# Self-attention: the softmax's division moved from the probabilities to the output block

## The reference, cut to what matters

```
s = jnp.einsum('bkgqd,bskd->bkgqs', q_blk, k).astype(jnp.float32) * scale
p = jax.nn.softmax(s, axis=-1).astype(v.dtype)
return jnp.einsum('bkgqs,bskd->bkgqd', p, v)
...
attn_branch = block_attention(q, k, v) @ w_attn_o
```

## Time and profile before

| | us |
|---|---|
| median of 3 runs | 2601.33 |
| lowest, highest | 2599.62, 2607.33 |
| profiled execution, its time | 2596.83 |
| its span | 2595.0 |

### The profile page before, as it was taken

One profiled execution on the slowest core, in us unless ns is written; L12 is line 12 of the kernel. 1 busy time (PEld: TensorE's weight loads), 2 busy tenths in 40 slices (PEclk: granted clock), 3 DMA queues, 4 the chain that ended last, 5 costly groups with the idle time before them and its releaser, 6 DMA issues.

```text
span 2595.0 us, 38678 instructions
## 1 busy us (share of the span) xinstructions
PE 2451.1 (94%) x13083; PEld 2070.5 (80%) x13083; DVE 2167.5 (84%) x3950; ACT 1101.6 (42%) x1943; POOL 1374.2 (53%) x1054
## 2 busy tenths in 40 slices
PE   7989999899989999999998889999999999999998
PEld 5767888788876778777866668888888888888887
DVE  6355544886779897877889978999999999999999
ACT  4464444333257313343317993333333333333333
POOL 0000000315832554745755547888887777777875
PEclk9999999999999999999999999999999999999999
DMA  6745545447974797877943559999999999999998
GB/s 249 267 139 179 195 146 181 174 189 262 381 270 119 290 333 289 337 271 254 387 167 134 211 223 391 414 415 415 415 415 415 415 414 415 415 415 394 415 415 317
DMA packets 240423, 787.50 MB, mean 303 GB/s; under 512 B 21905, under 2 KB 75329, under 8 KB 219553
## 3 DMA queue, kind: packets, MB, share of 16 engines
q0 software_dynamic: 112288, 408.77, 40.4%
q1 hardware_dynamic: 128000, 377.00, 39.0%
HBM read 728.01 MB, written 57.67 MB: 303 GB/s over the span
## 4 chain that ended last, share of the span: by engine, by line
PE 35%; DVE 23%; issue 20%; ACT 9%; DMA 9%; POOL 3%; POOLq 0%; DVEq 0%; SPq 0%; ACTq 0%
PE lin L245 9%; PE lin L247 9%; PE lin L246 9%; ACT row_ring L1866 4%; DVE Y L2494 3%; DVE w_lo L222 2%; DMA G<-in_downT 2%; DMA w_raw<-in_wall 2%; DVE rows L2480 2%; DVE row_ring L138 2%; DMA rows<-in_up,now 2%; DVE w_raw L2480 2%; DVE low L2460 2%; DVE low L2471 2%; PE tr L1795 2%
## 5 line engine op out<-in xcount | busy, mean ns | idle before, releaser
L150 POOL DMA_INDIRECT row_ring<-in_down,IDX x256 | 371.3, 1450 | 303.3 <-DVE dots L138 229.1
L222 DVE TENSOR_TENSOR w_lo<-w_raw,w_hi 128x2048 fp32r<-128x2048 f32 x100 | 229.2, 2292 | 218.5 <-ACT w_hi L214 214.1
L245 PE MATMUL lin<-w_hi,T_hi 128*128 128x512 f32 x976 | 389.0, 399 | 15.0 <-DVE w_lo L222 7.8
L247 PE MATMUL lin<-w_hi,T_lo 128*128 128x512 f32 x976 | 388.5, 398 | 0.0
L246 PE MATMUL lin<-w_lo,T_hi 128*128 128x512 f32 x976 | 386.1, 396 | 0.0
L214 ACT ACTIVATE w_hi<-w_raw 128x2048 fp32r<-128x2048 f32 x116 | 222.1, 1914 | 354.2 <-PE lin L247 331.5
L2353 POOL DMA_INDIRECT rows<-in_up,now x192 | 311.9, 1625 | 64.7 <-issue 56.8
L138 DVE CUSTOM_DVE_ANT_0 row_ring<-row_ring,H 128x1024 f32<-128x1024 f32 x256 | 303.0, 1223 | 37.9 <-DMA row_ring<-in_down,IDX 37.5
L245 PE MATMUL lin<-w_hi,c_hi 128*128 128x512 f32 x768 | 307.1, 400 | 15.9 <-DVE c_lo L2507 15.9
L2353 POOL DMA_INDIRECT w_raw<-in_up,now x189 | 274.2, 1451 | 84.2 <-issue 43.8
L245 PE MATMUL tr<-T_hi,w_hi 128*128 128x384 f32 x896 | 304.2, 340 | 2.2 <-DVE low L2460 2.2
(11 more groups left out here) (310 smaller groups left out, 5254.2 us busy)
## 6 DMA issues: line engine op xcount, KB each, us to landing
w_raw<-in_wall SPq DMA_DIRECT2D x116, 1024.0 KB, 6.8
row_ring<-in_up SPq DMA_DIRECT2D x128, 512.0 KB, 11.8
G<-in_downT SPq DMA_DIRECT2D x112, 512.0 KB, 11.3
wd<-dense_gates SPq DMA_DIRECT2D x32, 768.0 KB, 22.4
weight_rests<-w_lo SPq DMA_DIRECT2D x16, 1024.0 KB, 4.9
w_lo<-weight_rests SPq DMA_DIRECT2D x16, 1024.0 KB, 4.8
dense_gates<-peer SPq DMA_DIRECT2D x6, 2048.0 KB, 6.3
dense_gates<-w_raw SPq DMA_DIRECT2D x5, 2048.0 KB, 6.9
```

The lines of the kernel that those rows point to most:

```text
L150: pool.indirect_dma_start(self.ring[:, r % self.K, :], None, self.table, bass.IndirectOffsetOnAxis(ap=self.IDX[:, r:r + 1], axis=0)).then_ ...
L222: dve.tensor_tensor(self.lo[:, h % 2], self.raw[:, h % 2], self.hi[:, h % 2].bitcast(F32), ALU.subtract).then_inc(self.lo_done, 1)
L245: pe.matmul(out, lhs[0], rhs[0], start=start, stop=False, skip_group_check=True)
L247: return pe.matmul(out, lhs[1], rhs[0], start=False, stop=stop, skip_group_check=True)
```

## The change

The probabilities stay unnormalised. DVE's reciprocal and its two multiplications in every step go. Once for each block, DVE inverts all its sums (`invert`, in step `last + 1`), PE spreads the inverses over the block's 128 rows with small matmuls (`spread_factors`: the inverse of one tile and head, broadcast to 64 columns, as the stationary operand, the identity as the moving one), ACT copies the spread factors from the free bank of `tr` to `stage[2]`, DVE multiplies the block's output by them into `stage[0]` or `stage[1]`, ACT copies that into T_hi and DVE subtracts it for T_lo. The turn waits for the exponentials and no longer for DVE. The projection behind the attention no longer waits for all blocks at once but for each (`Blocks`). The background rows go to one in every step, and two in every third: 45 in the loop of the sample, where there were 26.

```
 class SelfAttention:
-    def norm(self, dve, p):
-        i = p % 3
-        dve.wait_ge(self.exped, 2 * p + 2)
-        dve.reciprocal(self.rr[:, i, :], self.rs[:, i, :]).then_inc(self.inverted, 1)
-        dve.wait_ge(self.inverted, p + 1)
-        for e in range(2):
-            dve.tensor_scalar(self.probs[:, i, e, 0:self.w], self.probs[:, i, e, 0:self.w], self.rr[:, i, e:e + 1], None,
-                              ALU.mult).then_inc(self.normed, 1)
+    def invert(self, dve, n):
+        nt = self.q.nt
+        dve.wait_ge(self.exped, 2 * nt * (n + 1))
+        dve.reciprocal(self.rr[:, n % 2, 0:nt, :], self.rs[:, n % 2, 0:nt, :]).then_inc(self.inverted, 1)
...
 def self_attention
+        LAG = 2 if q.nt == 4 else 3
+        last = [(hp + 1) * q.nt - 1 for hp in range(NH // 2)]
...
                 for e in range(2):
-                    pe.wait_ge(normed, 2 * p + e + 1)
+                    pe.wait_ge(exped, 2 * p + e + 1)
...
+            def spread_factors(n):
+                pe.wait_ge(att.inverted, n + 1)
+                if n >= 1:
+                    pe.wait_ge(scaled, n)
+                for t in range(q.nt):
+                    for e in range(2):
+                        product = pe.matmul(factors(n)[rows_of(e), t * P:(t + 1) * P],
+                                            att.rr[:, n % 2, t, e:e + 1].broadcast_to((P, HD)), ident[:],
+                                            start=True, stop=True, skip_group_check=True)
+                product.then_inc(valued, 1)
...
                 if step < N:
                     att.scores(pe, step)
+                for n, p in enumerate(last):
+                    if q.nt == 2 and step == p + LAG:
+                        spread_factors(n)
                 if 2 < step < N + 2:
                     turn(step - 2)
+                for n, p in enumerate(last):
+                    if q.nt == 4 and step == p + LAG:
+                        spread_factors(n)
                 if 3 <= step:
                     values(step - 3)
...
         @block.scalar
-                    if step == block_end[n] + 3:
-                        act.wait_ge(valued, 2 * block_end[n])
-                        act.activation(T[0][:, n, 0:w], tr[:, n % 2, 0:w], ACT.Copy).then_inc(out_hi, 1)
+                    if step == p + 3:
+                        act.wait_ge(valued, spread_done(n))
+                        if n == 0:
+                            spills_done(act)
+                        else:
+                            act.wait_ge(scaled, n)
+                        act.activation(factor(n), factors(n), ACT.Copy).then_inc(out_hi, 1)
+                    if step == p + 5:
+                        act.wait_ge(scaled, n + 1)
+                        act.activation(T[0][:, n, 0:w], out(n), ACT.Copy).then_inc(out_hi, 1)
...
         @block.vector
-                if 1 <= step < N + 1:
-                    att.norm(dve, step - 1)
-                if step % 4 != 0:
-                    bg.dve(dve, 1)
+                    if step == p + 1:
+                        att.invert(dve, n)
+                    if step == p + 4:
+                        dve.tensor_tensor(out(n), tr[:, n % 2, 0:w], factor(n), ALU.mult).then_inc(scaled, 1)
+                    if step == p + 6:
+                        dve.tensor_tensor(T[1][:, n, 0:w], out(n), T[0][:, n, 0:w].bitcast(F32),
+                                          ALU.subtract).then_inc(out_lo, 1)
+                if step < N + 4:
+                    bg.dve(dve, 2 if step % 3 == 0 else 1)
...
 def mixer_outputs
+            project_tokens(pe, st, H, 2, T, range(NT), lin, o, turn=blocks)
             attended(pe)
-            project_tokens(pe, st, H, 2, T, range(NT), lin, o)
```

More of the change, by code:

```diff
@@ L1074, in attention, with self_attention, factors, values_done @@
         return attended
-def self_attention(nc, block, q, bg, T, v_sb, ident, lin, tr, att, projected):
+def self_attention(nc, block, q, bg, T, v_sb, stage, ident, lin, tr, att, projected, spills_done):
     with ExitStack() as ctx:
         m = Pool(nc, ctx)
-        probs, rows_of, kv_of, normed, turned = att.probs, att.rows_of, att.kv_of, att.normed, att.turned
+        probs, rows_of, kv_of, exped, turned = att.probs, att.rows_of, att.kv_of, att.exped, att.turned
         pT = m.sb("att_probsT", [P, 2, 2, SAMPLE // P, P])
         copied, valued, out_hi, out_lo = (m.sem(f"att_{x}") for x in ("copied", "valued", "out_hi", "out_lo"))
+        scaled = m.sem("att_scaled")
+        LAG = 2 if q.nt == 4 else 3
         pairs, N, w = att.pairs, att.N, att.w
-        block_end = [(hp + 1) * q.nt for hp in range(NH // 2)]
+        last = [(hp + 1) * q.nt - 1 for hp in range(NH // 2)]
+        blocks = Blocks(out_lo)
+        def factors(n):
+            return tr[:, (n + 1) % 2, 0:w]
+        def values_done(p):
+            return 2 * (p + 1) + sum(x + LAG <= p + 3 for x in last)
+        def spread_done(n):
+            return 2 * (last[n] + LAG - 3) + n + 1
+        def fetched(n):
+            return 2 * n + 1
+        def hi_done(n):
+            return 2 * n + 2
+        def factor(n):
+            return stage[:, 2, 0:w]
+        def out(n):
+            return stage[:, n % 2, 0:w]
         @block.tensor
@@ L1096, in turn @@
                     for kb in range(q.nt):
-                        last = pe.transpose(lin[:, 4 + e, kb * P:(kb + 1) * P],
-                                            probs[:, p % 3, e, kb * P:(kb + 1) * P], ident[:])
-                    last.then_inc(turned, 1)
+                        product = pe.transpose(lin[:, 4 + e, kb * P:(kb + 1) * P],
+                                               probs[:, p % 3, e, kb * P:(kb + 1) * P], ident[:])
+                    product.then_inc(turned, 1)
             def values(p):
@@ L1129, in copy @@
                 if p >= 2:
[L1130 removed]
+                    act.wait_ge(valued, values_done(p - 2))
                 for e in range(2):
@@ L1167, in attended, with mixer_outputs @@
             eng.wait_ge(out_lo, NH // 2)
-        return attended
-def mixer_outputs(nc, block, st, q, bg, x_in, T, Y, G, lin, tr, A, U, GA, GS, ident, cleared, attended, spills_done):
+        return attended, blocks
+def mixer_outputs(nc, block, st, q, bg, x_in, T, Y, G, lin, tr, A, U, GA, GS, ident, cleared, attended, blocks, spills_done):
     NT, H = q.nt, q.h0 + 2 * W_AO
@@ L2575, in layer @@
                                                                    A, U, GA, GS, stage, ident, gains, *carried)
[L2576 removed]
+                        attended, blocks = self_attention(nc, block, q, bg, T, v_sb, stage, ident, lin, tr, att, projected,
+                                                          spills_done)
                     norm_m, mixed = mixer_outputs(
[L2578 removed]
+                        nc, block, st, q, bg, x_in, T, Y, G, lin, tr, A, U, GA, GS, ident, cleared, attended, blocks, spills_done)
                     with ExitStack() as c2:
```

56 lines of the change are left out of this document (33 added, 23 removed).

## The result

The changed kernel took 2613.23 us, median of 5 runs (2609.02 to 2617.14); the kernel before took 2601.33 us in 5 runs (2598.71 to 2607.33). The ratio is 1.0043, 95% interval 1.0025 to 1.0061: 11.9 us slower, where 2606 us, some 5 us slower, was forecast. The time lies inside the range and above the 0.3% bound. The profiled execution took 2609.02 us (span 2607.2), 12.2 us more than that of before.

A forecast was written before the change was run, and what follows sets the result against it. Two interleaved dependency rings (exponential, copies, turn, values, scores, maximum), no full engine, pace both loops. Sample +4.2, prompt +4.5, routing -3.6 give +5.1 us on 2596.83; 4.5 more for the median gives 2606 us, range 2595 to 2614.

The forecast's parts named there:

- rival B: Sample's loop: second rows of two-row steps delay the next maximum, +5.8 in place of 1.0, 2611 us; chance 0.20.
- +4.5 forecast: Prompt's loop: +5.4 us for seven longer blocks, less 0.9 of the projection's wait.
- 5.2 us against 4.43: Prompt's loop: a block takes 5.2 us, with PE itself in the dependency ring, against 4.43 before; +0.77.
- counted at -0.9: Prompt's loop end: the projection's wait of 0.97 us goes, 0.9 of it counted.
- +4.2 forecast: Sample's loop: 4.6 for seven blocks, +1.0 for the last block's spreading, -1.4 for the projection's wait.
- The spreading lies on the ring of the even steps: 14.26 us: Sample's loop: spreading between turn and values lengthens the even steps' dependency chain, 13.24 + 1.02 = 14.26 us a block.
- the other ring: Sample's loop: the odd steps' dependency chain, with two block copies on ACT in place of one, 14.20 us a block.
- 0.14 a block (1.0): Sample's loop: added for DVE in two-row steps with a block operation, 4.1 against 3.6 us; 7 x 0.14.
- +1.0 for the last spreading: Sample's loop end: the last block's spreading has no scores beside it to hide behind, +1.0 us.
- The projection's -1.4: Sample's loop end: the 1.45 us wait goes, since the projection's first half wants only blocks 0 to 3.
- -3.6 forecast: Routing: PE's 1.88 us wait and 1.68 us of slow clock go as 19 background rows leave.
- 0.6 us: Prompt's loop: one more TensorE drain per block from switching array tiling, 0.6 us over eight blocks, left out of the sum.

The follow-up runs named there:

- experiment 5: Changed kernel plus 20 dummy identity matmuls (4.4 us) in the pause before each loop's second turn; 2605.11 us, ratio 1.0013.
- experiment 12: Kernel before with blockwise projection, a background row in every step of the sample's loop and dummy matmuls in the pauses; 2592.71 us, ratio 0.9961.
- experiment 10: Kernel before with only the output projection waiting for blocks one by one; 2600.35 us, ratio 0.9991.
- Experiment 6: Changed kernel with only the first matmul of each block's spreading; 2608.46 us, ratio 1.0029.
- experiment 4: Changed kernel with 26 background rows in the sample's loop in place of 45; 2617.76 us, ratio 1.0063.
- in the second: Second trace, from the changed kernel run once more with nothing altered; 2617.54 us in one run.
- experiment 9: Kernel before with 34 dummy matmuls (8 us) ahead of the prompt's output projection; 2610.40 us, ratio 1.0037.
- experiments 3: Changed kernel with the sample's self-attention put back (normalised probabilities, 26 background rows), the prompt's as changed; 2616.44 us, ratio 1.0055.

## Why the prediction came out as it did

The sign of each part was right, and so were the prompt's block and the routing in size; by medians the loss was 11.9 us and not 5, and one step in the sample was right only in its number. That 2613 us lie in the range is partly luck: its upper end came from rival B, which came at a quarter of its price, and what carried the time there were the clock and a stretch that I had not priced.

*The prompt's loop, +4.5 forecast, +8.3 in the trace.* At full clock the loop takes 38.7 us (experiment 5) against 33.6 with the projection's wait (experiment 12): +5.1. The step "5.2 us against 4.43" holds to 0.03 us. But up to the last turn the loop loses only 4.6 us (199.43 - 164.01 = 35.42 against 195.74 - 164.91 = 30.83), not the 5.4 of seven blocks: the last two, which have few scores or none beside them, lose nothing (3.48 and 3.30 us between products, 4.25 and 2.75 between the T_lo before). The end, counted at -0.9, costs +0.5 (3.30 us from the last turn to the projection against 2.84): I had passed over it, and the last values wait 1.03 us for ACT. The remaining 3.2 us are clock. This is the term the sum lacked: I priced the loop as if the half-clock piece behind the pause had one length, and read 0.96 in the earlier trace rows as no concern of the change. With the new loop PE stands still 0.85 us in each block and the piece lasts 8.8 to 11.7 us; its cost is 3.3 to 4.7 us in place of 1.4 (1.9 in experiment 10). That keeping PE at work takes it away is shown; why the new loop keeps it longer, by its stalls or by its later matmuls, was not separated.

*The sample's loop, +4.2 forecast, +5.5 in the trace.* "The spreading lies on the ring of the even steps: 14.26 us" is the step that failed. What binds is the other ring: 13.24 + 2 x 0.48 = 14.20, with one block copy on each half of it. ACT's timeline of the changed kernel has both, three exponentials of the odd steps and three of the even ones:

```profile
795.07 0.69 ACT L660 ACTIVATE att_probs<-lin,att_sums 128x512 f32<-128x512 f32 x1 [0.66 <-DVE att_sums L665]
802.20 0.69 ACT L660 ACTIVATE att_probs<-lin,att_sums 128x512 f32<-128x512 f32 x1 [1.17 <-DVE att_sums L665]
809.30 0.69 ACT L660 ACTIVATE att_probs<-lin,att_sums 128x512 f32<-128x512 f32 x1 [0.69 <-DVE att_sums L665]
...
769.92 0.69 ACT L660 ACTIVATE att_probs<-lin,att_sums 128x512 f32<-128x512 f32 x1 [3.21 <-DVE att_sums L665]
777.41 0.69 ACT L660 ACTIVATE att_probs<-lin,att_sums 128x512 f32<-128x512 f32 x1 [1.47 <-DVE att_sums L665]
784.02 0.69 ACT L660 ACTIVATE att_probs<-lin,att_sums 128x512 f32<-128x512 f32 x1 [0.26 <-DVE att_sums L665]
```

The odd ones are 7.13 and 7.10 us apart, each 6.62 + 0.48 within 0.03: 14.23 us. The even ones are 7.49 and 6.61 us apart, 14.10 us: the spreading costs its ring 0.87 us and not 1.02, for it starts 0.93 us ahead of the values, which then take 0.97 us up to the scores in place of 1.02. Experiment 6 shows the same from the other side: cutting the spreading left 14.24. Two rings 0.14 us apart hid the error; I took the one for the cause that my sum made 0.06 us the longer. The spreading costs only together with a step of two rows, as these lines in the long block show:

```profile
816.45 1.09 PE L1160 MATMUL tr<-ident,att_sums 128*64 128x128 f32 x16
...
819.55 1.23 DVE L665 TENSOR_REDUCE att_sums<-lin 128x2 f32<-128x1024 f32 x1 [1.41 <-PE lin L645]
820.69 1.22 DVE L138 CUSTOM_DVE_ANT_0 row_ring<-row_ring,H 128x1024 f32<-128x1024 f32 x1
...
821.83 1.22 DVE L138 CUSTOM_DVE_ANT_0 row_ring<-row_ring,H 128x1024 f32<-128x1024 f32 x1
...
822.98 1.22 DVE L665 TENSOR_REDUCE att_sums<-lin 128x2 f32<-128x1024 f32 x1
```

The spreading makes one maximum late, two rows follow it, and the next maximum, of the ring that binds, starts straight behind them with no idle time. It took 0.69 us in two of six distances, 1.4 us, where 0.14 a block (1.0) was counted; taking away either partner, the rows (experiment 4) or the spreading (6), ends it. The long blocks are not those I named by their block operations, and the delay fades, so B's 5.8 us did not come.

The end of the loop was mis-sized too: "+1.0 for the last spreading". At full clock it is 863.96 - 859.15 = 4.8 us from the last turn to the projection, against 857.87 - 854.95 = 2.9 (experiments 5 and 12), +1.9: the spreading, 0.93, and the factor copy ahead of the last turned copy, which the ring's arithmetic had shown me in the prompt's loop and which I did not carry to the end. The projection's -1.4 came. So the 5.5 us are 7.5 blocks from the second turn to the last at 0.49 (3.7), the long blocks (1.4) and the end (4.8 us against 4.4 before, 0.4).

*The routing, -3.6 forecast, -4.2 in the trace* (-3.5 in the second), of which the wait and the slow piece are 3.7 in both. They went together, and the waits came back with the 26 rows.

*Not in the forecast, and open:* the +3.9 us between the prompt's projection and the sample's first scores. This stretch took 519.8 to 527.8 us in eight traces with the new prompt's loop, and 521.4 to 525.9 in six with the old one. Part of it is a load, `G<-in_mem`: from its issue to the first reader 6.4 us, 5.25 before. This is no mark of the change: it took 5.1 to 5.5 us in seven of the fourteen traces and 6.3 to 6.8 in the other seven, with both loops in each group. By the medians of experiment 9 lateness is not the cause either. But the medians of experiments 3 and 4 lie 4 to 7 us above the sum of their traces' parts, so a share of the change in this stretch can't be excluded.

*Drains.* The rule of the Trainium skill that I weighed (TensorEngine Tiling (Array Packing), Key Properties) would have added 0.6 us at the price that I took from the rows. The prompt's distance of 5.17 us leaves no room for it on top of the 5.2 counted; no run here isolates a drain.

## What to carry to other kernels

Where two rings of dependencies come out alike, the forecast of the time may hold and its cause be wrong; read each ring's own starts, and expect little more from cutting the longer than its lead over the other (0.18 us a block here, with a lead of 0.14). Follow a queue's new entries to the last iteration, where nothing overlaps them. And a pause of some microseconds ahead of a latency-bound loop is worth filling with dummy matmuls: here 8 us in the new scheme and 3 to 4 in the old, by medians.

## What the runs showed of the hardware

- Behind the same 4.9 us pause TensorE ran at half its clock for 3.2 to 6.3 us in one loop and for 8.8 to 11.7 in another, in which it stands still 0.85 us once in each block; 4.7 us of dummy matmuls in the pause left no such piece in either, and delayed nothing.
- One fp32 matmul of 128 columns ahead of a dependent copy costs 0.47 us until the copy starts, four cost 0.70: of a short group most is latency, and making it shorter gives little.
- An ACT copy of one column takes 0.20 us against 0.62 for 512 columns, and took 0.42 us (7.13 to 6.71) off two of three passes that it stood on; in the third a two-row step left 0.11 of it.
